# Tokens turned by VectorE, and a fourth buffer for the high parts of expert weights, in a hybrid encoder layer with sixteen experts

## The reference, cut to what matters

```python
logits = (tok @ router_w)
aff = jax.nn.softmax(logits, axis=-1)
gate, idx = lax.top_k(aff.T, cap)            # per sequence, cap = 64
xs = tok[idx]                                # 16 x 128 x 1024 over both sequences
hid = silu(einsum('ecd,edf->ecf', xs, w_gate)) * einsum('ecd,edf->ecf', xs, w_up)   # f = 1408
ye = einsum('ecf,efd->ecd', hid, w_down) * gate[..., None]
out = zeros_like(tok).at[idx.reshape(-1)].add(ye.reshape(-1, D))
```

## Time and profile before

| what | value |
|---|---|
| median of 3 runs | 1491.75 us |
| span of the profiled execution | 1489.4 us |
| median less that span | 2.4 us |
| TensorE (PE) busy | 1467.0 us, 99% |
| VectorE (DVE) busy | 1189.5 us, 80% |
| ScalarE (ACT) busy | 819.8 us, 55% |
| granted TensorE clock, mean | 0.996 |
| moved by DMA | 388.26 MB, mean 261 GB/s |

### The profile page before, as it was taken

How to read it: one execution, slowest core, us unless ns; L and a number is a source line. 1 busy time by engine, 2 the same in 40 slices (tenths; PEclk the granted TensorE clock), 3 DMA queues, 4 the chain that set the end, 5 groups by cost and what they waited for, 6 DMA issues and landing times.

```text
span 1489.4 us, 18913 instructions
## 1 busy us (share of the span) xinstructions
PE 1467.0 (99%) x7042; PEld 1235.5 (83%) x7042; DVE 1189.5 (80%) x1024; ACT 819.8 (55%) x777; POOL 167.3 (11%) x119
## 2 busy tenths in 40 slices
PE   9999999999999999998999999999999999999996
PEld 8878888888888888888888888888888888888885
DVE  5688988896767766346888888888888888888886
ACT  6322232123622222333677777777777777777776
POOL 1000001000005200011110112011110121012101
PEclk9999999999999999999999999999999999999998
DMA  7210232623263255677999999999999999999997
GB/s 236 58 43 0 81 87 75 224 85 99 94 230 121 87 183 197 227 253 283 347 362 365 376 376 374 384 374 377 374 377 381 377 374 374 384 376 376 374 374 286
DMA packets 220971, 388.26 MB, mean 261 GB/s; under 512 B 8603, under 2 KB 87771, under 8 KB 220412
## 3 DMA queue, kind: packets, MB, share of 16 engines
q1 hardware_dynamic: 213692, 361.39, 68.4%
q0 software_dynamic: 7232, 26.22, 5.8%
HBM read 348.78 MB, written 38.80 MB: 260 GB/s over the span
## 4 chain that ended last, share of the span: by engine, by line
PE 71%; DVE 2%; DMA 0%; issue 0%; ACT 0%; POOLq 0%; POOL 0%; ACTq 0%
PE ps L1779 23%; PE ps L1781 22%; PE ps L1780 22%; PE ps L2162 1%; PE ps L2154 1%; PE ps L2199 1%; PE ps L2082 0%; PE ps L2064 0%; DMA slot_tokens<-tok_rows,rows_to_gather 0%; DVE top_index L1651 0%; DVE affinity_rows L1654 0%; DVE top_of_halves L1647 0%; DVE expert_lo L1207 0%; DVE tok_rows L1592 0%; ACT expert_hi L804 0%
## 5 line engine op out<-in xcount | busy, mean ns | idle before, releaser
L1207 DVE TENSOR_TENSOR expert_lo<-expert_raw,expert_hi 128x2048 fp32r<-128x2048 f32 (+1 forms) x285 | 597.5, 2110 | 92.1 <-ACT expert_hi L804 91.1
L804 ACT ACTIVATE expert_hi<-expert_raw 128x2048 fp32r<-128x2048 f32 (+1 forms) x285 | 506.5, 1778 | 177.8 <-PE ps L1781 174.0
L1779 PE MATMUL ps<-expert_hi,slot_tokens_T_hi 128*128 128x512 f32 (+1 forms) x768 | 289.8, 377 | 2.0 <-DVE slot_tokens_T_lo L1207 1.0
L1780 PE MATMUL ps<-expert_lo,slot_tokens_T_hi 128*128 128x512 f32 (+1 forms) x768 | 285.2, 371 | 0.0
L1781 PE MATMUL ps<-expert_hi,slot_tokens_T_lo 128*128 128x512 f32 (+1 forms) x768 | 285.2, 371 | 0.0
L1779 PE MATMUL ps<-hT_hi,w_hi 128*128 128x512 f32 x576 | 226.2, 393 | 1.0 <-DVE hT_lo L1219 1.0
L1781 PE MATMUL ps<-hT_hi,w_lo 128*128 128x512 f32 x576 | 224.3, 389 | 0.0
L1780 PE MATMUL ps<-hT_lo,w_hi 128*128 128x512 f32 x576 | 224.2, 389 | 0.0
L1779 PEld LDWEIGHTS ps<-expert_hi,slot_tokens_T_hi 128*128 128x128 f32 x768 | 144.1, 188 | 25.1 <-issue 4.0
L1781 PEld LDWEIGHTS ps<-expert_hi,slot_tokens_T_lo 128*128 128x128 f32 x768 | 144.2, 188 | 20.4
L1241 DVE SCALAR_TENSOR_TENSOR conv_sum<-a_padded,small_params,conv_sum 128x1024 f32<-128x1024 f32 x120 | 158.1, 1317 | 3.4
(11 more groups left out here) (314 smaller groups left out, 1843.6 us busy)
## 6 DMA issues: line engine op xcount, KB each, us to landing
expert_raw<-in_w_gate SPq DMA_DIRECT2D x64, 1024.0 KB, 8.7
expert_raw<-in_w_up SPq DMA_DIRECT2D x64, 1024.0 KB, 8.6
expert_raw<-in_w_down SPq DMA_DIRECT2D x64, 1024.0 KB, 8.1
expert_raw<-in_w_gate SPq DMA_DIRECT2D x32, 768.0 KB, 7.5
expert_raw<-in_w_up SPq DMA_DIRECT2D x32, 768.0 KB, 7.2
expert_raw<-in_w_down SPq DMA_DIRECT2D x32, 768.0 KB, 8.5
w_raw<-in_w_in SPq DMA_DIRECT2D x36, 512.0 KB, 4.8
gate_in<-gate_spill SPq DMA_DIRECT2D x22, 512.0 KB, 3.9
```

Source lines behind the costliest of these rows:

```text
L804: nc.scalar.activation(out, src, ACT.Copy, **scale).then_inc(s, 1)
L1207: V.tensor_tensor(out, src, high_part.bitcast(F32), ALU.subtract).then_inc(s, 1)
L1779: nc.tensor.matmul(out, a[0], b[0], start=first, stop=False)
L1780: nc.tensor.matmul(out, a[0], b[1], start=False, stop=False)
```

## The change

Tokens of experts 1 to 15 turned by VectorE, and a fourth buffer for the high parts of expert weights, paid for by narrower raw slots for 384-column blocks. What it does:

- **The turn.** VectorE's transpose works within blocks of 32 partitions by 32 columns. The gather is therefore cut in four indirect DMAs that bring quarter rows of 1 KB (128 each), so that each group of 32 partitions holds the quarter of the rows that it needs; `PIECES` holds their indices, four times the row plus the quarter. One VectorE transpose of 128x1024 (`turn_tokens`, in unit 13 of the body before) then gives `turned_tokens` in SBUF. ScalarE and VectorE make high and low parts from it ahead of unit 0 of the expert's body. The contracted rows end up eight neighbouring rows to a partition, and the gate and up weights are loaded in that order (`"o (p t) n -> p (o t) n"`); the size and the number of their packets stay.
- **Expert 0** keeps its gather and TensorE's transposes, with columns taken in the new order. Four small copies by ScalarE (`FOUR_TIMES`), four small transposes by TensorE (`slot_pieces`) and one VectorE operation make the indices.
- **Buffers.** `SPLITS = 4`: units 6 to 17 of a body use a buffer last used four or more units before, units 0 to 5 one used three before, as now (`HI_ORDER`). Four raw slots that only hold 384-column blocks have 6 KB per partition. `XS` moves.
- **Order.** TensorE transposes the last hidden block before it waits for `xsT_lo`. `gate_out` moves behind the split of unit 9. GpSimd issues gather(e + 1) ahead of scatter(e - 1). The load of `NGF` moves from the start of the experts to SP's place between the last weights and the accumulated rows, because `turned_tokens` has its space.

```diff
-        raw_at = [174, 182, 190, 198, 40, 104, 112, 80, 88, 96, 120, 128, 8, 16, 24, 32, 164, 72]
+        raw_at = [174, 182, 190, 198, 40, 104, 112, 80, 88, 96, 120, 126, 8, 14, 20, 28, 164, 72]
+        NARROW = range(10, 14)
...
         FLYING = 3
-        EW = [at(f"expert_raw{j}", k, [P, 4, 512]) for j, k in enumerate(raw_at)]
-        SPLITS = 3
-        ES = [at(f"expert_hi{j}", 48 + 8 * j, [P, 4, 512], F32R) for j in range(SPLITS)]
-        EL = [at(f"expert_lo{j}", k, [P, 4, 512], F32R) for j, k in enumerate(raw_at)]
-        XS = at("slot_tokens", 136, [P, D])
+        EW = [at(f"expert_raw{j}", k, [P, 4, 384 if j in NARROW else 512]) for j, k in enumerate(raw_at)]
+        SPLITS = 4
+        ES = [at(f"expert_hi{j}", k, [P, 4, 512], F32R) for j, k in enumerate((48, 56, 64, 132))]
+        EL = [at(f"expert_lo{j}", k, [P, 4, 384 if j in NARROW else 512], F32R) for j, k in enumerate(raw_at)]
+        XS = at("slot_tokens", 36, [P, D])
+        XS_BY_TILE = XS[:].rearrange("p (n k) -> p k n", k=KD)
+        TURNED = at("turned_tokens", 160, [P, KD, P])
...
             w = w_gate if kind == "gate" else w_up
-            return w[bass.ds(e, 1), k * 4 * P:(k + 1) * 4 * P, a:a + n].rearrange(
-                "o (t p) n -> p (o t) n", p=P), 4, n
+            return w[bass.ds(e, 1), :, a:a + n].rearrange(
+                "o (p t) n -> p (o t) n", p=P)[:, 4 * k:4 * k + 4, :], 4, n
...
         FIRST = [n for n in range(NB) if not LEAD <= n < LEAD + SKIPPED]
-        assert NB % RAWS == 0 and NB % SPLITS == 0
+        assert NB % RAWS == 0
+        HI_ORDER = (0, 1, 2, 3) * 3 + (0, 1, 2) * 2
+        HI_OF = [HI_ORDER[(n - 3) % NB] for n in range(NB)]
+        assert all(FC[BODY[n][1]][1] <= 384 for n in range(NB) if (n - SKIPPED) % RAWS in NARROW)
+        def hi_free(n, e):
+            order = FIRST if isinstance(e, int) and e == 0 else range(NB)
+            at_n = pos(n, e)
+            for before in range(at_n - 1, -1 if order is FIRST else at_n - NB - 1, -1):
+                if HI_OF[order[before % len(order)]] == HI_OF[n]:
+                    return before + 1
+            return None
...
                     sp.wait_ge(acc_stored, 16 * TT)
-                    sp.dma_start(NGF[:], norm_f_g.to_broadcast([P, D])).then_inc(norm_g_in, 16)
...
+            sp.wait_ge(xsT_lo, E)
+            sp.dma_start(NGF[:], norm_f_g.to_broadcast([P, D])).then_inc(norm_g_in, 16)
...
-                if not isinstance(e, int):
-                    pool.wait_ge(xs_in, e * 16)
-                    pool.wait_ge(xsT_mm, e)
-                pool.wait_ge(slots_ready, 2)
-                nc.gpsimd.tensor_copy(NEXT_ROWS[:], SLOTS[:, bass.ds(e, 1)]).then_inc(rows_next, 1)
+                pool.wait_ge(xs_in, (e - 1) * 64 + 16)
+                ge(pool, xs_turned, e)
+                pool.wait_ge(slots_ready, 5)
+                nc.gpsimd.tensor_copy(NEXT_PIECES[:], PIECES[:, bass.ds(e, 1), :].rearrange("p o a -> p (o a)")).then_inc(rows_next, 1)
...
                 pool.wait_ge(rows_next, e)
-                pool.indirect_dma_start(XS[:], None, tok_dram,
-                                        bass.IndirectOffsetOnAxis(ap=NEXT_ROWS[:], axis=0)).then_inc(xs_in, 16)
+                for a in range(4):
+                    pool.indirect_dma_start(XS[:, a * 256:(a + 1) * 256], None, tok_pieces,
+                                            bass.IndirectOffsetOnAxis(ap=NEXT_PIECES[:, a:a + 1], axis=0)).then_inc(xs_in, 16)
...
-                if not isinstance(e, int):
+                if not (isinstance(e, int) and e == 0):
...
             pool.wait_ge(pads_set, 5)
-            pool.wait_ge(xs_in, 16)
-            pool.wait_ge(xsT_mm, 1)
             gather(1)
+            gather(2)
             scatter(0)
-            with pool.Fori(1, E - 1) as e:
+            with pool.Fori(2, E - 1) as e:
                 gather(e + 1)
-                scatter(e)
+                scatter(e - 1)
+            scatter(E - 2)
+            pool.wait_ge(slots_ready, 2)
+            nc.gpsimd.tensor_copy(NEXT_ROWS[:], SLOTS[:, E - 1:E]).then_inc(rows_next, 1)
+            pool.wait_ge(rows_next, E)
             pool.wait_ge(added, 16 * (E - 1))
-            pool.wait_ge(xs_in, 16 * E)
-            pool.wait_ge(xsT_mm, E)
+            pool.wait_ge(xs_in, 64 * (E - 1) + 16)
+            pool.wait_ge(xsT_lo, E)
...
                 act.wait_ge(e_landed[r], landed_of(n, e))
-                ge(act, e_used, base + pos(n, e) - SPLITS + 1)
-                q = pos_mod(n, e, SPLITS)
+                if hi_free(n, e) is not None:
+                    act.wait_ge(e_used, base + hi_free(n, e))
+                q = HI_OF[n]
...
                     high(XST[0][:, 0:4, :].rearrange("p k n -> p (k n)"), PS[:, 6, :], rows_ready)
-                    act.wait_ge(xsT_mm, e + 1)
+                    act.wait_ge(xs_turned, e + 1)
...
                     return
-                act.wait_ge(xsT_mm, e + 1)
-                high(XST[0][:].rearrange("p k n -> p (k n)"), PS[:, 6:8, :].rearrange("p a n -> p (a n)"), xsT_hi)
+                act.wait_ge(xs_turned, e + 1)
+                act.wait_ge(e_used, e * NB - SKIPPED - len(down_units(1)))
+                high(XST[0][:].rearrange("p k n -> p (k n)"), TURNED[:].rearrange("p k n -> p (k n)"), xsT_hi)
...
                 for n in range(NB):
+                    if n == 0 and not first:
+                        xsT_high(e)
...
                             nc.scalar.activation(LISTS[:, g, 0, :], TOP[32 * g:32 * g + E, :], ACT.Copy).then_inc(rows_ready, 1)
-                    if n == (2 if first else 0):
+                    if first and n == 2:
+                        act.wait_ge(pair_ready, 1)
+                        for a in range(4):
+                            part = nc.scalar.activation(FOUR_TIMES[:, a, :, :], PAIR[:, 1, 32 * a:32 * a + 32][:, None, :].to_broadcast([E, 4, P // 4]),
+                                                        ACT.Copy)
+                        part.then_inc(rows_ready, 1)
+                    if first and n == 2:
...
                         silu(0, e, base)
-                    if n == 8 and not first:
-                        gate_out(e - 1, base + LEAD + 1)
...
                         hidT_high(0, e, base)
+                    if n == 9 and not first:
+                        gate_out(e - 1, base + LEAD + 1)
...
                 if isinstance(e, int) and e == 0:
-                    dve.wait_ge(rows_ready, 6)
+                    dve.wait_ge(rows_ready, 7)
...
                         XST[0][:, 4:8, :].rearrange("p k n -> p (k n)"), xsT_lo)
+                    dve.wait_ge(slots_mm, 3)
+                    V.tensor_scalar(PIECES[:].rearrange("p e a -> p a e"), PS[:, 4, 0:4 * E].rearrange("p (a e) -> p a e", a=4),
+                                    4.0, QUARTER[:], ALU.mult, ALU.add).then_inc(slots_ready, 1)
...
                 dve.wait_ge(xsT_hi, e + 1)
-                low(XST[1][:].rearrange("p k n -> p (k n)"), PS[:, 6:8, :].rearrange("p a n -> p (a n)"),
+                low(XST[1][:].rearrange("p k n -> p (k n)"), TURNED[:].rearrange("p k n -> p (k n)"),
                     XST[0][:].rearrange("p k n -> p (k n)"), xsT_lo)
+            def turn_tokens(e):
+                dve.wait_ge(xs_in, e * 64 + 16)
+                V.transpose(TURNED[:], XS_BY_TILE).then_inc(xs_turned, 1)
+            TURN_AT = 13
...
                 for n in range(NB):
+                    if n == 0 and not first:
+                        xsT_low(e)
...
                         split_e(n, e, base)
-                    if n == (1 if first else 0):
+                    if first and n == 1:
...
                         hidden(1, e, base)
+                    if n == TURN_AT and not last:
+                        turn_tokens(e + 1)
...
+            def slot_pieces():
+                pe.wait_ge(rows_ready, 6)
+                for a in range(4):
+                    mm = nc.tensor.transpose(PS[:, 4, a * E:(a + 1) * E], FOUR_TIMES[:, a, :, :].rearrange("e b n -> e (b n)"),
+                                             IDENT[0:E, 0:E])
+                mm.then_inc(slots_mm, 1)
...
                 for k in range(KD):
-                    mm = nc.tensor.transpose(PS[:, 6 + k // 4, (k % 4) * P:(k % 4 + 1) * P], XS[:, k * P:(k + 1) * P], IDENT)
+                    mm = nc.tensor.transpose(PS[:, 6 + k // 4, (k % 4) * P:(k % 4 + 1) * P], XS_BY_TILE[:, k, :], IDENT)
...
                         mm.then_inc(affT_mm, 1)
-                mm.then_inc(xsT_mm, 1)
+                mm.then_inc(xs_turned, 1)
...
                 else:
-                    tokens_of(e + 1)
                     down(1, e, down_counts(1, e, base))
+                    hidden_T(2, e)
                     pe.wait_ge(xsT_lo, e + 2)
-                    hidden_T(2, e)
...
             keep_busy(22)
+            slot_pieces()
```

(15 more changed lines are left out.)

## The result

The changed kernel takes **1494.17 us** (median of 11 runs, 1493.23 to 1496.86), the kernel before, on the same chip, 1491.3 us. The ratio is 1.002, with a 95% interval of 1.0013 to 1.0028: slower, by 0.13 to 0.28%. The forecast was 1488.2 us, a gain; the time lies 0.2 us outside the range of 1483.5 to 1494.0. The two profiled executions stand 1492.4 to 1489.4 us, so +3.0 us, about what the medians say (+2.9).

What follows compares the result with a forecast made beforehand. TensorE and DMA were both taken as near their limit, the tail waiting for TensorE with 7.7 us of slack before DMA. -7.7 - 1.8 + 1.3 + 1.6 + 3.1 = -3.5 us gave 1488.2 us, range 1483.5 to 1494.0.

Steps and rivals of the forecast that it cites:

- What bounds the kernel: Expert stage: TensorE runs without a gap, DMA needs 48.7 us per expert against 47.8; transposes cost TensorE 12.0 us.
- The slack of the loads is 7.7 us: Tail: first accumulated rows land 7.7 us before ScalarE squares them, the most the end can come forward; -7.7 us.
- -1.8 us: Weight stream up to 808 us: TensorE's lead frees slots earlier and two unsaturated stretches fill; -1.8 us.
- The norm's load, +1.3: Tail: the final norm's 512 KB load now stands between the last weights and the accumulated rows; +1.3 us.
- The late gather ahead of the last weights, +1.6: Tail: TensorE's lead brings the late gather of accumulated rows ahead of the last weights; 1.3 to 2.4, taken as +1.6 us.
- Pieces, 0.24 us an expert: DMA stream: each gather becomes 512 packets of 1 KB at 49 ns; 0.24 us each, thirteen times, +3.1 us.
- B (nearly free): Gather pieces: four 1 KB packets take what one of 4 KB takes; sum -6.6 or -8.2 us; chance 0.17.
- C (dear): Gather pieces: at 57 ns a packet they cost 6.5 us, sum -0.1, time 1491.7 us; chance 0.18.
- Rival D: Gate and up loads slow down in the new row order: gain gone at 0.9%, 1496 us at 2%; chance 0.10.
- Rival E: The turn is slow on VectorE: no idle time left from about 4.8 us, 1504 us at 6.5; chance 0.03.
- my 1.2: VectorE: one 128x1024 transpose per expert was taken to need 1.2 us and to fit its 5.7 us idle.
- GpSimd issues four gathers in place of one ... 0: GpSimd's queue: four gathers of 2.55 us each land within the body that issues them, a turn before use; 0.

Runs made afterwards that it cites:

- order_one_transpose: The kernel before with one TensorE transpose instead of eight for experts 1 to 15, and the change's order of high and low tokens: 1487.07 us, ratio 0.9972.
- three_buffers: The changed kernel with three buffers for high parts in turn instead of four, as the kernel before has: 1493.45 us, ratio 1.001.
- row_order: The kernel before with only the gate and up weights loaded in the change's row order: 1491.43 us, ratio 1.0.

## Why the prediction was wrong

The step that failed and turned the sign is the last of this list: the four gathers in place of one were put at 0 on GpSimd's queue, and they cost 3.53 us in the drain. Without them the time would be 1490.6 us by estimate, still 2.4 over the forecast: that part is the slack of 7.7 us, which took the tail behind the first rows as fixed, and the stream's costs, which were put too low.

- **What bounds the kernel**: right. TensorE lost 12.1 us (12.0 forecast), the chain went over to DMA, the stock ran out, the last square stopped waiting for TensorE. "The stream doesn't get faster by freeing TensorE" is the centre of the result.
- **"The slack of the loads is 7.7 us"**: wrong, the largest term of the forecast. I measured from the landing of the first rows to their use and forgot that the same engines carry the other loads, the late gather and eight stores. The stream's room is the idle time up to the last store that it can fill, 4.0 us. order_one_transpose, which pays neither for pieces nor for the norm's load in the tail, gained 4.4.
- **"-1.8 us" of recovered idle time**: wrong in sign. The old gaps gave back 1.3 us by their shares (1.7 forecast for both), but expert 0's buffer order opened one of 2.3 us and the norm's place at the start stayed empty: 2.5 us more idle time in all. The prediction looked at the fourth buffer in the loop ("units 6 to 17") and not at the expert that skips two units.
- **The norm's load, +1.3**: the load takes that (last weight 1461.62, `norm_f_g_all` 1462.90), but on a stream that is full to the end only bytes and idle time count; its cost is the time left idle at the start, by the packets 1.1 us.
- **The late gather ahead of the last weights, +1.6**: it did move (issued 1447.82 instead of 1454.12), but it lies ahead of the last store either way, so it is no term.
- **Pieces, 0.24 us an expert**: 0.21 measured, and 3.1 us forecast for thirteen. Right in size by luck, wrong in kind: I argued with packets of 1 KB, which the trace doesn't have, and with a line that 2 KB and 4 KB "lie on", as any two points do. B (nearly free) and C (dear) don't hold.
- **Rival D** falls by row_order. **Rival E** falls too, though the turn takes 2.20 us and VectorE is busy 45.2 of 48 us in the loop. The estimate from "VectorE: DVE Perf Modes" of the Trainium skill ("The three transpose paths"), 2.5 us, was nearer than my 1.2.
- **"GpSimd issues four gathers in place of one ... 0"**: the step that cost most, and with it the sign. In GpSimd's queue the issue is hidden, but the 45 DMAs more come back in the drain at the end, +3.53 us. That drain stood in the trace of before, behind the last landing; I read the tail only to VectorE's last operation and took what follows as fixed.

How the spans add up, by bytes: up to 1440 us the changed kernel has moved 1.74 MB less, at 377 GB/s 4.6 us: 0.81 MB by 856 us (idle time) and 0.93 MB since (pieces). The 4.0 us of room in the tail take up most of it: the last store is 0.25 us late, and some 0.35 us between 0.6 and 0.25 I can't place.

The prediction's own steps lead to the same place. By them the first rows were to land 4.2 us later than before (-1.8 + 1.3 + 1.6 + 3.1); they landed 6.3 us later (1464.17 against 1457.88), the last weights 5.0 us (1461.62 against 1456.62) and the norm's load 1.3. Against that stood the 7.7 us. But from the use of the first rows to the last store the kernel before took 17.16 us (1465.56 to 1482.72), while the stream, once it sets the pace, needs 18.8: 1464.17 to 1482.97 here, 1458.87 to 1477.66 in order_one_transpose, 1461.87 to 1480.67 in three_buffers. So 6.29 + 1.64 - 7.68 = 0.25 us late: the stream's costs were 2.1 us too small, and the tail behind the first rows wasn't a fixed length.

GpSimd's first scatter of the two is issued at 1480.74, 1.5 us earlier. The second waits for the last store, is issued 0.28 us earlier than before (1483.23 against 1483.51) and lands 0.54 us earlier. Then the drain, +3.53: together +3.0. So the gain was absorbed (the stream had 4.0 us of room and was charged 4.6), and what made the kernel slower was the drain. Open is why closing the gap in expert 0 brings less than it closes.

## What to carry to other kernels

Where a stream of transfers is full, measure the room in the tail as idle time of the DMA engines up to the last store that further transfers can fill, with the stores counted, not as the gap between one landing and its use. Read a trace to its very last instruction: here the drain that closes GpSimd's block grew with the number of DMAs that GpSimd had issued, and one drain where GpSimd stands idle took 2.5 us off the kernel before and 4.7 off the changed one. When a ring of buffers is lengthened, walk its order through the peeled iteration too.

## What the hardware showed that I had not expected

- GpSimd's drain reaches 2.18 us behind the last landing with 52 DMAs, 5.7 with 97 (78 ns for each of the 45 between), 0.12 when a drain has come before; 45 DMAs of 64 bytes count as much as 45 gathers.
- Four indirect gathers of 1 KB pieces are recorded in packets of 4 KB, as one gather of whole rows is; they still cost 0.21 us more an expert.
- While 45 DMAs of 16 packets of 4 bytes ran, the stream moved 159 to 183 GB/s instead of 377 at a full share, by estimate 0.3 us for each.
- A 128x1024 transpose of 32-bit values on VectorE takes 2.20 us, where a multiplication by a column takes 0.75 and a subtraction 1.22 us.
